# Two pool products emptied ahead of weight splits, and one group's running sums moved, in a two-block recurrent and attention kernel

## The chip, the cores and the metric

The kernel runs on one core of a Trainium2 chip. The metric is the device time of one execution in microseconds (us). Before the change it is 1481.7 us, the median of three runs (1480.57 to 1482.08).

## The reference, cut to what matters

Two transformer-like blocks follow each other on 528 positions (16 meta tokens and 512 real ones) of width 1024, in 32-bit floats. Only the first half of the first block matters here:

```python
z = rmsnorm(h, norm1_g)
q, fl, iv, og, pin, ga, gb = jnp.split(z @ w_in, SPLITS, axis=-1)
o_a = hgrn2_mixer(q, fl + b_f, iv, og, lb_all, head_norm_g)   # 8 heads, gated recurrence
o_b = pool_mixer(pin, w_pool, pool_scale)                     # 4 groups of 128 channels
mix = sigmoid(ga) * (o_a @ w_branch_a) + sigmoid(gb) * (o_b @ w_branch_b)

# pool_mixer, for group g with window w = (2, 4, 8, 16)[g]:
#   d = trailing_mean(pin[:, g], w) - pin[:, g];  y = (d @ w_pool[g]) * pool_scale
```

## The kernel before, in words

**Precision.** Each 32-bit operand of a large product is split in a high and a low part; a product is the sum of three TensorE products (high·high, high·low, low·high). Weights come in units of 1024 KB: SyncE loads a unit to `raw`, ScalarE copies it to `whi` (the high part), and VectorE subtracts to get `wlo` (`w_low`, line 1900). TensorE may start a tile only when `wlo` of its unit is done (`w_lo`).

**Tiles and slots.** The projection `z @ w_in` is worked off in tiles of 128 output channels by all positions; a tile is eight steps of three products in two halves, 48 matmuls of 258 or 264 columns (line 908). Its result lies in one of two PSUM slots, taken in turn. A tile may start only after the one before in its slot was emptied (`acc_free`). The four pool products (`("pool", g)`, six matmuls each) take their turns in the same two slots. A pool product is emptied twice over: ScalarE writes the scaled high part `obhi`, then VectorE writes the low part `oblo` (`pool_out`, line 2155), and only that frees the slot.

**The order.** It is one list, `order`, that TensorE, ScalarE and VectorE each walk through by hand-written rules. The recurrence works on pairs of heads p = 0 to 3; its ten steps (i = 0 to 9) are hung as hooks on the tiles. In the stretch around the change the tiles are, with their hooks (p, i) in brackets: og0 (1,4), pool0, og1 (1,5), pool1, og2 (1,6), pool2, og3 (1,7) and (1,8), q6 (1,9) and (2,0), q7 (2,1), pool3, f6 (2,2), f7 (2,3), g00 (2,4), and so on (q6 is `("q", 6)`, g00 is `("g", 0, 0)`). The slots: og1, og2, og3, q7 and f6 use slot 0; pool1, pool2, q6, pool3 and f7 use slot 1.

**TensorE's side.** After a tile it carries out the hooks. Steps (p,1) to (p,7) are small matmuls on `E` (lines 1009 to 1043) that wait for `mul_ready`. Step (p,9) (lines 1075 and 1077) starts with a wait for `qd_ready`, and at its first chunk for `c0_copied`; it signals `o_done`. Step (p+1,0) follows (transposes, line 988).

**VectorE's side, in its order.** At og1: hooks, then `pool_prep(2)` (running sums on line 2168, the mean minus the frame on line 2174, the split to `pdhi` and `pdlo` on lines 2182 and 2184, with the recurrence's products of step 6 in between), then the low part of the weights of unit q6. At pool1: `pool_out(1)`. At og2: differences of step 7 (lines 2046 and 2047), a masked copy, products of step 7 (lines 2058 and 2059). At pool2: `pool_out(2)`. At og3: a masked copy, the low part of the weights of unit f6, and the differences of step (2,0) (lines 2038 and 2041). At q6: copies of scores (lines 2073 to 2083), the five small masked copies to `sc0` that end in `c0_copied` (lines 2144 and 2149), the products of step (2,0), and, once `o_done` of p = 1 is there, the differences of step (2,1). Then `pool_prep(3)`: four running sums, products of step (2,1), which wait for ScalarE's exponentials, the mean, the split. At q7: differences and products of step (2,2), and the low part of the weights of unit g00. At pool3: `pool_out(3)`.

A unit is handed to `w_low` at the last tile of the unit two places ahead in the order; the dictionary `end_of` says at which tile:

```python
w_low(*end_of.get(name, ()))
```

ScalarE's own walk through the list (the high parts of the weights at `first_of`, table loads, exponentials, `obhi`) isn't touched.

Of the kernel before, what the change touches and what calls it, by code (L numbers as in the profile page):

```python
# [34 lines left out]
T = NM + SEQ  # L35
# [8 lines left out]
POOL_WINDOWS = (2, 4, 8, 16)  # L44
PADC = 16
# [247 lines left out]
def build_program(nc: bass.Bass, a, out):  # L293
# [3 lines left out]
    with ctx:  # L297
        def at(name, shape, dt, offset):
            size = int(np.prod(shape[1:])) * {F32: 4, F32R: 4, BF16: 2, U8: 1}[dt]
            return nc.alloc_sbuf_tensor_at(name, shape, dt, offset=offset), offset + size  # L300
# [54 lines left out]
        og, e = at("og", [P, 4, T], F32, e)  # L355
        pin, e = at("pin", [P, 4, T + PADC], F32, e)
# [12 lines left out]
        pp = [at(f"pp{i}", [P, T + PADC], F32, GOFF + i * (T + PADC) * 4)[0] for i in range(2)]  # L369
# [216 lines left out]
        def acc_late(name):  # L586
            s = 2 * pl.tile[name][0]
            return PS[:, s:s + 2, 0:LHALF]

        def halves(t):  # L590
            return t.rearrange("p (a b) -> p a b", a=2)

        def late(t):
            return t[:, LATE:T]

        def tile_done(eng, name):
            eng.wait_ge(pe_mark, pl.tile[name][1])

        def tile_free(ins, name):
            ins.then_inc(acc_free[pl.tile[name][0]], 1)  # L600

        def tile_freed(eng, name):
            slot, _, uses = pl.tile[name]
            eng.wait_ge(acc_free[slot], uses + 1)
# [42 lines left out]
        first_of, end_of = {}, {}  # L647
# [172 lines left out]
        def _(pe):  # L820
# [39 lines left out]
            def gemm_steps(name, free=True):  # L860
# [5 lines left out]
                s = pl.slot[p.unit]  # L866
                pe.wait_ge(w_lo, p.unit + 1)
                slot, _, uses = pl.tile[name]
                if p.first and uses and free:
                    pe.wait_ge(acc_free[slot], uses)  # L870
# [516 lines left out]
        def _(act):  # L1387
# [25 lines left out]
            def w_high(*units):  # L1413

                for u in units:
                    assert u == n_high[0], (u, n_high)
                    n_high[0] += 1
                    _, kt, cols = pl.units[u]
                    s_ = pl.slot[u]
                    act.wait_ge(w_landed[s_], landed_at[u])  # L1420
                    A_(hi[s_][:, 0:kt * cols], raw[s_][:, 0:kt * cols], ACT.Copy).then_inc(w_hi, 1)
# [457 lines left out]
        def _(dve):  # L1879
# [3 lines left out]
            def tick(ins):  # L1883
                steps[0] += 1
                ins.then_inc(dve_step, 1)

            def settle():
                dve.wait_ge(dve_step, steps[0])
# [3 lines left out]
            def w_low(*units):  # L1892

                for u in units:
                    assert u == n_low[0], (u, n_low)
                    n_low[0] += 1
                    _, kt, cols = pl.units[u]
                    s_, n_ = pl.slot[u], kt * cols
                    dve.wait_ge(w_hi, u + 1)
                    V.tensor_tensor(lo[s_][:, 0:n_], raw[s_][:, 0:n_], hi[s_][:, 0:n_].bitcast(F32), ALU.subtract)\  # L1900
                     .then_inc(w_lo, 1)
# [104 lines left out]
            def values_out(j, turned, copied, dst, m, c0):  # L2006
                dve.wait_ge(turned, j + 1)
                r0 = 96 if m == QB else 0
                V.tensor_copy(dst[r0:r0 + NM, m, P * j:P * (j + 1)], PS[0:NM, 5, 0:P]).then_inc(copied, 1)
                V.tensor_copy(dst[:, c0:c0 + 4, P * j:P * (j + 1)], PS[:, 4, :].rearrange("p (c f) -> p c f", c=4))\  # L2010
                 .then_inc(copied, 1)
# [140 lines left out]
            def pool_out(g):  # L2152
                n = ("pool", g)
                dve.wait_ge(obhi_ready, g + 1)
                tile_free(V.scalar_tensor_tensor(out=halves(late(oblo[:, g, :])), in0=acc_late(n), scalar=col("pscale", g),
                                                 in1=halves(late(obhi[:, g, :].bitcast(F32))), op0=ALU.mult,
                                                 op1=ALU.subtract), n)

            def pool_prep(g, between=lambda: None):

                W_, w = T + PADC, POOL_WINDOWS[g]
                tile_freed(dve, ("pin", g))
                src = pin[:, g, :]
                cur = src
                for s in range(g + 1):
                    d = 1 << s
                    dst = pp[s % 2]
                    tick(V.tensor_tensor(dst[:, 2 * d - 1:W_], cur[:, 2 * d - 1:W_], cur[:, d - 1:W_ - d], ALU.add))
                    settle()
                    cur = dst  # L2170
                between()
                dst = pp[(g + 1) % 2]
                c0 = PADC + w - 1
                tick(V.scalar_tensor_tensor(out=dst[:, c0:W_], in0=cur[:, c0:W_], scalar=1.0 / w, in1=src[:, c0:W_],
                                            op0=ALU.mult, op1=ALU.subtract))
                tick(V.tensor_tensor(dst[:, PADC:c0], cur[:, PADC:c0], inv_n[:, 0:w - 1], ALU.mult))
                settle()
                tick(V.tensor_tensor(dst[:, PADC:c0], dst[:, PADC:c0], src[:, PADC:c0], ALU.subtract))
                settle()
                if g >= 2:  # L2180
                    tile_done(dve, ("pool", g - 2))
                tick(V.tensor_copy(pdhi[g % 2][:, :], dst[:, PADC:W_]))
                settle()
                V.tensor_tensor(pdlo[g % 2][:, :], dst[:, PADC:W_], pdhi[g % 2][:, :].bitcast(F32), ALU.subtract)\
                 .then_inc(pd_ready, 1)
                dve.wait_ge(pd_ready, g + 1)

            def branch_b(k):
                n = ("y", 0, k)
                tile_done(dve, n)  # L2190
                tile_freed(dve, ("g", 0, k))
                tile_free(V.tensor_tensor(halves(late(mix[:, k, :])), acc_late(n), halves(late(mix[:, k, :])), ALU.mult), n)

            waiting = []
            for name, hooks in order:
                kind, h = name[0:2]
                p, hh = h // 2, h % 2
                for step in (hooks if kind != "y" else []):
                    rec_step(*step)
                p_, i_ = hooks[-1] if hooks else (0, 0)  # L2200
                if waiting and name != ("v", 1):
                    values_out(waiting.pop(0), v_turned, v_copied, vtok1, 0, 1)
                if kind == "v":
                    waiting.append(h)
                if name == ("y", 0, 0):
                    rec_step(3, 9)
                    branch_b(0)
                if kind == "f":
                    tile_freed(dve, name)
                    if p >= 2:  # L2210
                        dve.wait_ge(o_done, 2 * (p - 1))
                    f, k_ = av[p % 2][:, hh, :], kf[p % 2][:, hh, :]
                    tick(V.tensor_scalar(f, k_, omlb[:, h:h + 1], lb[:, h:h + 1], ALU.mult, ALU.add))
                    settle()
                    V.tensor_scalar(k_, f, -1.0, 1.0, ALU.mult, ALU.add).then_inc(f_ready, 1)
                    if 1 <= i_ <= 6:
                        rec_step(p_, i_ + 1, "products")
                        rec_step(p_, i_ + 1, "state and differences")
                    dve.wait_ge(ln_ready, h + 1)
                    V.tensor_tensor_scan(f, rmask[:, :], f, 0.0, ALU.mult, ALU.add).then_inc(a_ready, 1)  # L2220
                if name == ("pin", 2):
                    dve.wait_ge(spilled, 16)
                    pool_prep(0)
                elif name == ("q", 4):
                    pool_prep(1)
                elif name in (("og", 1), ("q", 6)):
                    pool_prep(2 if kind == "og" else 3, lambda: rec_step(p_, i_ + 1, "products"))
                elif kind == "pool":
                    pool_out(h)
                if kind != "f" and name != ("og", 1) and 1 <= i_ <= 6:  # L2230
                    rec_step(p_, i_ + 1, "products")
                w_low(*end_of.get(name, ()))
                if i_ == 8 and p_ < 3:
                    rec_step(p_ + 1, 0, "differences")
# [449 lines left out]
```

## Time and profile before

| | us |
|---|---|
| median of 3 runs | 1481.7 (1480.57 to 1482.08) |
| profiled execution, its own time | 1483.7 |
| its span, first to last instruction | 1481.5 |
| TensorE busy in the span | 1460.8 |
| VectorE busy | 839.4 |
| ScalarE busy | 699.8 |
| mean granted TensorE clock | 0.997 of full |

The span is what the trace shows; the 2.2 us between it and the execution's own time lie outside of the first and last instruction. Busy shares are means over stages; a wait counts only where TensorE, which is busy nearly all the time, stands still for it.

### The profile page before, as it was taken

Reading aid. Unit: us, or ns where it says so; the run is one execution under the profiler, and the core shown is the slowest. Engines: PE = TensorE matmul, PEld = TensorE weight load, DVE = VectorE, ACT = ScalarE, POOL = GpSimd, SP = SyncE. Lnnn points to the kernel's source line nnn. Section 1 sums busy time; section 2 is a strip of 40 time slices with the busy share of each in tenths; the row PEclk is TensorE's granted clock in tenths of the full one; section 3 lists DMA queues with packets and bytes.
Section 4 is the critical chain, followed back from the end, with each engine's and each line's share of the span. In section 5 each row is a group of like instructions: output and inputs, shape, how many; then the busy total and the mean of one; then the engine's idle time right before and its main releaser. Section 6 shows DMA issues by size and latency. Waiting matters only on the chain.

```text
span 1481.5 us, 26488 instructions
## 1 busy us (share of the span) xinstructions
PE 1460.8 (99%) x11375; PEld 1293.3 (87%) x11375; DVE 839.4 (57%) x1365; ACT 699.8 (47%) x1041; POOL 51.9 (4%) x150
## 2 busy tenths in 40 slices
PE   7999999999999999999999999999999999999998
PEld 7999999999999899898888777788899888778888
DVE  6487877764656566653344888542223666643343
ACT  6475877853443222222333677532122877743232
POOL 0000000000000000000000021000000111100000
PEclk9999999999999999999999999999999999999999
DMA  6222121124422233223234300222223111123222
GB/s 233 97 65 88 58 85 61 59 72 139 134 86 87 85 100 100 86 86 106 81 100 108 63 29 1 77 90 91 85 86 91 58 58 58 58 90 95 86 94 78
DMA packets 134871, 126.03 MB, mean 85 GB/s; under 512 B 24521, under 2 KB 132836, under 8 KB 134500
## 3 DMA queue, kind: packets, MB, share of 16 engines
q1 hardware_dynamic: 134084, 120.39, 26.1%
q0 software_dynamic: 656, 3.96, 0.9%
q8 instruction: 90, 1.47, 0.4%
q14 instruction: 25, 0.20, 0.0%
q10 hardware_dynamic: 16, 0.00, 0.0%
HBM read 119.69 MB, written 4.26 MB: 84 GB/s over the span
## 4 chain that ended last, share of the span: by engine, by line
PE 91%; DVE 3%; ACT 3%; issue 2%; DMA 0%; SPq 0%; DVEq 0%; ACTq 0%
PE PS L908 79%; PE PS L1242 2%; PE PS L1209 2%; PE PS L1190 2%; DVE wlo L1900 1%; ACT whi L1396 1%; PE PS L1194 1%; PE PS L1193 1%; PE PS L1019 1%; ACT Pm L1396 1%; DMA xt<-in_x 0%; PE PS L1219 0%; ACT L1396 0%; PE PS L975 0%; PE PS L1075 0%
## 5 line engine op out<-in xcount | busy, mean ns | idle before, releaser
L908 PE MATMUL PS<-zhi,whi 128*128 128x258 f32 (+2 forms) x1856 | 487.8, 320 | 2.5 <-DVE prm L1978 0.8
L908 PE MATMUL PS<-zhi,wlo 128*128 128x258 f32 (+2 forms) x1856 | 477.6, 315 | 0.0
L908 PE MATMUL PS<-zlo,whi 128*128 128x258 f32 (+2 forms) x1856 | 476.2, 315 | 0.6 <-DVE zlo L1948 0.6
L908 PEld LDWEIGHTS PS<-zhi,whi 128*128 128x128 f32 x1856 | 307.5, 189 | 27.4 <-issue 1.9
L908 PEld LDWEIGHTS PS<-zhi,wlo 128*128 128x128 f32 x1856 | 306.2, 189 | 22.3
L908 PEld LDWEIGHTS PS<-zlo,whi 128*128 128x128 f32 x1856 | 306.5, 189 | 20.9 <-DVE zlo L1948 0.8
L1900 DVE TENSOR_TENSOR wlo<-raw,whi 128x2048 fp32r<-128x2048 f32 (+2 forms) x114 | 247.8, 2174 | 119.3 <-ACT whi L1396 119.1
L1396 ACT ACTIVATE whi<-raw 128x2048 fp32r<-128x2048 f32 (+2 forms) x114 | 207.5, 1820 | 151.5 <-DMA raw<-in_w_up 57.3
L1396 ACT ACTIVATE Pm<-Pm,small 128x144 f32<-128x144 f32 (+3 forms) x128 | 73.1, 572 | 38.1 <-DVE small L2463 37.7
L2463 DVE CUSTOM_DVE_ANT_0 Pm<-PS,cmask 128x144 f32<-128x144 f32 (+3 forms) x128 | 62.9, 503 | 29.1 <-PE PS L1194 17.2
L908 PE MATMUL PS<-glo,whi 128*128 128x512 f32 x176 | 69.9, 397 | 0.0
L908 PE MATMUL PS<-ghi,whi 128*128 128x512 f32 x176 | 69.7, 396 | 0.0
L908 PE MATMUL PS<-ghi,wlo 128*128 128x512 f32 x176 | 69.1, 392 | 0.0
L1396 ACT ACTIVATE nsq<-PS 128x512 f32<-128x512 f32 x32 | 19.1, 596 | 102.5 <-PE PS L908 101.4
L1209 PE MATMUL PS<-ident,Pm 128*128 128x128 f32 x320 | 54.0, 274 | 1.8 <-ACT PT L1396 1.0
L803 POOL COPY Pe<-Pm 128x16 f32<-128x16 f32 x128 | 44.9, 354 | 224.7 <-ACT Pm L1396 216.8
L1209 PEld LDWEIGHTS PS<-ident,Pm 128*128 128x128 f32 x320 | 39.9, 140 | 14.7 <-ACT PT L1396 3.3
L1396 ACT ACT_TABLE_LOAD x37 | 47.5, 1283 | 7.8 <-PE PS L908 7.2
L908 PE MATMUL PS<-ylo,whi 128*128 128x512 f32 x128 | 51.1, 399 | 0.0
L908 PE MATMUL PS<-yhi,whi 128*128 128x512 f32 x128 | 50.4, 394 | 0.0
L908 PE MATMUL PS<-yhi,wlo 128*128 128x512 f32 x128 | 50.2, 392 | 0.0
L1396 ACT ACTIVATE E<-E 128x1056 f32<-128x1056 f32 (+2 forms) x32 | 33.5, 1048 | 31.7 <-DVE E L2047 26.7
(361 smaller groups left out, 2094.6 us busy)
## 6 DMA issues: line engine op xcount, KB each, us to landing
raw<-in_w_in SPq DMA_DIRECT2D x50, 1024.0 KB, 5.2
raw<-in_w_up SPq DMA_DIRECT2D x22, 1024.0 KB, 5.1
raw<-in_w_out SPq DMA_DIRECT2D x8, 1024.0 KB, 5.1
raw<-in_w_down SPq DMA_DIRECT2D x8, 1024.0 KB, 5.1
raw<-in_w_br_mla SPq DMA_DIRECT2D x4, 1024.0 KB, 5.1
raw<-in_w_br_fox SPq DMA_DIRECT2D x4, 1024.0 KB, 5.1
raw<-in_w_down SPq DMA_DIRECT2D x4, 768.0 KB, 4.5
hspill<-hT SPq DMA_DIRECT2D x1, 2112.0 KB, 7.6
```

Of the source, the lines that this page charges most:

```text
L803: nc.gpsimd.tensor_copy(Pe[h % 2][:, 32 * i:32 * i + NM], Pm[h % 2][:, o_:o_ + NM])\
L908: ins = mm(o_, l_, r_, start=first, stop=last)
L1019: ins = mm(dst.rearrange("p (n b) -> p n b", b=half), e[:, hh, t0 + r:t0 + r + 32], rhs, start=True, stop=True)
L1190: ins = mm(dst, qh[h % 2][:, t0:t0 + P], kh[h % 4][:, c0:c1], start=True, stop=True)
L1193: mm(dst, xqa[i_][:, t0:t0 + P], xka[i_][:, c0:c1], start=True, stop=False)
L1194: ins = mm(dst, xqb[i_][:, t0:t0 + P], xkb[i_][:, c0:c1], start=False, stop=True)
L1209: ins = tr(PS[:, 2 + g % 2, P * x:P * (x + 1)], Pm[h % 2][:, o_:o_ + P], ident[:, :])
L1242: mm(PS[64 * r:64 * r + 64, 7, P * j:SEQ], vtok[:, j, v0:v0 + DV], PT[r][:, G_COL[j]:G_COL[j] + G_N[j]], start=j == 0, stop=False, skip_gr ...
L1396: return nc.scalar.activation(out_, in_, func, **kw)
L1900: V.tensor_tensor(lo[s_][:, 0:n_], raw[s_][:, 0:n_], hi[s_][:, 0:n_].bitcast(F32), ALU.subtract)\
L2463: V.tensor_tensor_reduce(out=cut(Pm[h % 2][:, ATT_OFF[i]:ATT_OFF[i] + ATT_N[i]]), in0=s_view(i), in1=cut(cmask[:, T - ATT_N[i]:T]), op0=AL ...
```

## The change

VectorE's instructions are the same in kind and number; only their order changes.

- The low part of unit q6's weights moves from og1 to pool1, behind `pool_out(1)`.
- The low part of unit g00's weights moves from q7 to pool3, behind `pool_out(3)`.
- The low part of unit f6's weights moves from og3 to q6, behind all of `pool_prep(3)`.
- The four running sums of group 3 move from `pool_prep(3)` at q6 to og3, where the split of unit f6 stood.

```diff
-            def pool_prep(g, between=lambda: None):
+            def pool_sums(g):
 
-                W_, w = T + PADC, POOL_WINDOWS[g]
+                W_ = T + PADC
                 tile_freed(dve, ("pin", g))
                 src = pin[:, g, :]
                 cur = src
...
                     settle()
                     cur = dst
+
+            def pool_prep(g, between=lambda: None):
+
+                W_, w = T + PADC, POOL_WINDOWS[g]
+                if g < 3:
+                    pool_sums(g)
+                src, cur = pin[:, g, :], pp[g % 2]
                 between()
...
+            for early, later in ((("og", 1), ("pool", 1)), (("q", 7), ("pool", 3)), (("og", 3), ("q", 6))):
+                end_of[later] = end_of.pop(early)
             waiting = []
...
                     pool_prep(2 if kind == "og" else 3, lambda: rec_step(p_, i_ + 1, "products"))
+                elif name == ("og", 3):
+                    pool_sums(3)
                 elif kind == "pool":
                     pool_out(h)
```

## Rows read from the trace of the kernel before

**Rows 1.** The page's first part: busy us (share of the span) xinstructions.

```profile
PE 1460.8 (99%) x11375; PEld 1293.3 (87%) x11375; DVE 839.4 (57%) x1365; ACT 699.8 (47%) x1041; POOL 51.9 (4%) x150
```

**Rows 2.** Waits of TensorE: who waited for whom, total us, times, longest.

```profile
PE PS L908 <- DVE oblo L2155: 2.1, 1, 2.1
PE PS L908 <- DVE pdlo L2184: 0.7, 1, 0.7
PE PS L908 <- ACT qf L1396: 0.3, 1, 0.3
```

**Rows 3.** Stretches: length, busy us of each engine, then granted clock, DMA share, GB/s.

```profile
30.00:203.00 173.00, 169.47 (x2440) 165.14 (x2440) 129.18 (x205) 112.17 (x121) 0.00 (x0) 1.00 0.28 88
203.50:206.50 3.00, 3.00 (x15) 3.00 (x15) 0.89 (x2) 2.65 (x3) 0.00 (x0) 0.50 0.41 142
207.00:1460.00 1253.00, 1249.30 (x8642) 1088.63 (x8641) 681.09 (x1110) 560.48 (x867) 50.56 (x138) 1.00 0.27 81
```

**Rows 4.** Timeline of TensorE, 174 to 218: start us, us, instructions, [idle before <-releaser].

```profile
174.56 0.70 PE L1024 MATMUL PS<-E 128*32 128x32 f32 x32
177.32 0.48 PE L908 MATMUL PS<-pdhi,wphi 128*128 128x258 f32 x2 [2.06 <-DVE oblo L2155]
...
191.23 0.29 PE L1075 MATMUL PS<-sc,vtok 16*64 16x16 f32 x4
...
200.13 0.23 PE L1009 MATMUL PS<-E 128*16 128x8 f32 x3
...
202.01 0.51 PE L908 MATMUL PS<-pdhi,wphi 128*128 128x258 f32 x2 [0.69 <-DVE pdlo L2184]
...
217.89 0.23 PE L1009 MATMUL PS<-E 128*16 128x8 f32 x3
```

**Rows 5.** Timeline of VectorE, 174 to 191.

```profile
174.21 2.29 DVE L1900 TENSOR_TENSOR wlo<-raw,whi 128x2048 fp32r<-128x2048 f32 x1
176.42 0.75 DVE L2155 SCALAR_TENSOR_TENSOR oblo<-PS,prm,obhi 128x516 fp32r<-128x516 f32 x1
177.09 0.68 DVE L2046 TENSOR_TENSOR E<-av 128x512 f32<-128x512 f32 x1
...
181.88 0.76 DVE L2155 SCALAR_TENSOR_TENSOR oblo<-PS,prm,obhi 128x516 fp32r<-128x516 f32 x1 [1.08 <-ACT obhi L1396]
...
183.17 2.27 DVE L1900 TENSOR_TENSOR wlo<-raw,whi 128x2048 fp32r<-128x2048 f32 x1
185.37 0.18 DVE L2038 TENSOR_TENSOR E<-av 128x32 f32<-128x32 f32 x1
...
190.81 0.18 DVE L2149 COPY_PREDICATED sc<-lvl,PS 16x32 f32<-16x32 uint8 x1
```

**Rows 6.** Timeline of VectorE, 193 to 217.

```profile
193.50 0.71 DVE L2046 TENSOR_TENSOR E<-av 128x528 f32<-128x528 f32 x1 [1.59 <-PE PS L1077]
...
194.75 0.72 DVE L2168 TENSOR_TENSOR pp<-pin 128x543 f32<-128x543 f32 x1
195.50 2.22 DVE L2168 TENSOR_TENSOR pp<-pp 128x541 f32<-128x541 f32 x3
198.52 0.71 DVE L2058 TENSOR_TENSOR E<-E,qf 128x528 f32<-128x528 f32 x1 [0.79 <-ACT E L1396]
...
201.25 0.71 DVE L2184 TENSOR_TENSOR pdlo<-pp,pdhi 128x528 fp32r<-128x528 f32 x1
...
205.61 0.71 DVE L2058 TENSOR_TENSOR E<-E,qf 128x528 f32<-128x528 f32 x1 [2.29 <-ACT E L1396]
...
209.07 0.75 DVE L2155 SCALAR_TENSOR_TENSOR oblo<-PS,prm,obhi 128x516 fp32r<-128x516 f32 x1
...
214.42 0.55 DVE L2213 TENSOR_SCALAR av<-kf,small 128x528 f32<-128x528 f32 x1 [1.93 <-ACT kf L1396]
...
215.97 0.70 DVE L2059 TENSOR_TENSOR E<-E,kf 128x528 f32<-128x528 f32 x1
```

**Rows 7.** Chain that ended last: tiles f6, f7 and g00 (start us, us, what).

```profile
203.33 7.59 PE PS L908 x48
...
211.92 6.04 PE PS L908 x48
218.96 6.02 PE PS L908 x48
```

## The prediction

> **What bounds the kernel now.** Read the page's first part, TensorE's waits, and then the timelines of the few microseconds in which the change sits. TensorE is busy 1460.8 of 1481.5 us [rows 1]: any time that the change wins or loses is a shift of TensorE's instructions, and what VectorE does matters only where TensorE stands still for it. In the touched stretch TensorE waits three times [rows 2]: 2.1 us for `oblo`, 0.7 us for `pdlo`, 0.3 us for `qf`. There is one more loss. The granted clock is 1.00 from 30 to 203, 0.50 from 203.5 to 206.5, and 1.00 again from 207 to 1460 [rows 3], so tile f6 takes 7.59 us where f7 takes 6.04 [rows 7]: 1.55 us at the lower level (1.2 instead of 2.4 GHz). All that the change could win here is 2.1 + 0.7 + 0.3 + 1.55 = 4.6 us.
>
> **Part 1, `pool_out(1)` ahead of the split of unit q6.** TensorE's small matmuls of step (1,6) start at 174.56 and end at 175.26; pool2 starts at 177.32, 2.06 us later, because slot 1 is freed by the `oblo` of 176.42 [rows 4, 5]. That `oblo` stood behind the split of 174.21. The swap starts it at 174.21 and ends it at 174.96, before TensorE needs it. TensorE reaches pool2 at 175.2, 2.1 us early. VectorE's pair still ends where the differences start, at 177.09, so from there VectorE is as before: `oblo` of pool2 at 181.88 (it waits for ScalarE's `obhi`) and og3's work at 183.17 [rows 5]. Slot 1 is free for q6 at 182.64 + 0.15; TensorE wants it at 183.1 (its tile times unchanged). No wait there, by 0.3 us. Split q6 ends 0.7 us later than before, 6 us ahead of its need.
>
> **Part 2, sums in place of the split of f6 at og3.** The sums take from 194.75 to 197.72, 3.0 us [rows 6]. The split that they replace takes 2.2 (183.17 to the next start, 185.37) [rows 5]. From there to the end of the last copy to `sc0` (190.81 + 0.18 = 190.99) VectorE has no idle time, so `c0_copied` comes 0.8 us later, at 191.79. Step (1,9) waits for it; it starts at 191.23 now, right behind its tile, only 0.24 us after the copy's end [rows 4]. With Part 1 TensorE is there at 191.23 − 2.1 = 189.1 and finds nothing: it stands for 2.8 us and starts at 191.79 + 0.15 = 191.94 (0.15 is what lies between the end of `oblo` at 177.17 and pool2 at 177.32). So the 2.1 us of Part 1 are lost again (2.0 of them would be lost even without Part 2), and 0.7 us on top. A split or a sum in place of the other between two idle ends would cost nothing; here the cover is gone. Bounds: 0.65 to 0.85, by a release of 0.05 (`pdlo` at 201.96 to pool3 at 202.01) or 0.15 and sums of 2.95 to 3.0.
>
> **Part 3, the same sums removed at q6.** The differences of 193.50 follow `o_done`, so they shift by 0.7 to 194.2. The sums that stood behind them were followed by 0.79 us of idle before the products of 198.52, which wait for ScalarE's exponential [rows 6]. ScalarE's chain (the copy of `oT`, two table loads, silu, exponential) also starts at `o_done`, so the products go to 199.2, not earlier. Taking 3.0 us of sums away makes the idle time longer and nothing else. `pdlo`, 201.25 + 0.71 = 201.96 now, ends at 202.67. TensorE still waits for it before pool3.
>
> **Part 4, the split of f6 behind `pool_prep(3)`.** It was done at 185.4; f6 starts at 203.33 [rows 7]. Now it can only start when `pdlo` ends: 202.70 + 2.27 = 204.97, and f6 starts at 205.1. This is the new wait, 1.8 us after 203.33 (0.7 of it carried from Part 2, 1.1 new); the 0.3 us for `qf` disappear in it. Behind the split VectorE has the differences of step (2,2), 202.0 now, 204.9 then; ScalarE's exponential of them, and the products of 205.61, which come at about 207.3. TensorE needs these products only after f6. Lower end for this part: 0 beyond the carried 0.7, if VectorE got the split done in its idle time ahead of the products; its order forbids it. Upper end 1.2. I take 1.1, the durations being shown.
>
> **Part 5, `pool_out(3)` ahead of the split of g00.** The `oblo` of 209.07 frees slot 1 for f7, which starts at 211.92, and no wait stands there [rows 6, 7]: worth 0 now. It is of use against Part 4: VectorE is 1.7 us late at the products, the `oblo` comes at 208.6 (not 209.07 + 1.7), and what follows it is 1.6 us late. The split of g00 ends at 211.4; g00 starts at 218.96. ScalarE's `kf` follows the same delay: 214.42 becomes about 216.05.
>
> **The sum.** −2.1 (Part 1) + 2.1 (stands before step (1,9)) + 0.7 (Part 2) + 0 (Part 3) + 1.1 (Part 4) + 0 (Part 5) = +1.8 us at the start of f6. If f6 again takes 7.6 us, f7, g00 and all behind shift by 1.8: VectorE is late by 1.6 and so isn't the bound. From 230 on TensorE meets nothing that isn't itself counted from TensorE's own tiles, so the shift stays to the end. Profiled execution: 1483.7 + 1.8 = 1485.5. The median of the runs stands 2.0 under the profiled execution; the forecast is 1481.7 + 1.8 = 1483.5 us, a loss of 0.12%. I take 0.2% (3.0 us) as what can be told from no change, so this counts as no change.
>
> **The clock, row and rule.** The row: TensorE stood 2.06 us at 175.26 and the clock stayed at 1.00; it fell to 0.50 after the small matmuls of 200.13, a stop of 0.69, pool3 and a stop of 0.33 [rows 2 to 4]. So one stop of 2 us didn't do it, and thin work with short stops did. The Trainium skill ("TensorE: Matmul & The Clock Gate", section "HAM oscillation — how this bites in real kernels") says that waits between bursts put the array back to half clock and that the next burst starts cold. By this rule the new stand of 2.8 us ahead of step (1,9) speaks against the change; by the row it may pass. With the rule the forecast would be that of rival A, with the row that of the sum.
>
> **Rivals.** *A, the clock halves at step (1,9) (slower).* TensorE stands 2.8 us, longer than any stop in the stretch; if the clock then falls, step (1,9), from 191.23 to the differences' start at 193.50 (2.25 us), loses between 0.5 and 2.2 us, and everything hangs on its `o_done`: differences, exponential, `pdlo`, split, f6. Middle +1.7: 1483.5 + 1.7 = 1485.2 us. Half clock in tile q7 behind it costs nothing, for TensorE waits for `pdlo` and the split anyway. For it: the length of the stop, and that step's matmuls are short. Against: the stop at 175.26. It decides from 1.2 us of extra time up. *B, the clock doesn't fall at f6.* The stops around it change place. f6 then takes 6.0 instead of 7.6, and TensorE would be at step (2,3) ahead of VectorE: its products now end at 216.67 for a start at 217.89 [rows 4, 6], 1.2 us of slack against a delay of 1.6. Shift +0.5: 1482.2 us. *C, faster: the copies to `sc0` don't hold step (1,9).* If the release of step (1,9) were another, earlier one, and VectorE's work from 183 to 191 had slack, the 2.1 us of Part 1 would stay up to `o_done`, `pdlo` would come 2.1 us earlier and the split end at 202.1, ahead of f6: −2.1, and −1.55 more with a full clock: 1479.6 or 1478.0 us. For it: no wait is recorded there now. Against: TensorE comes just 0.24 us after the copy's end. *D, the reorder does nothing that TensorE sees* (±0.4, 1481.7): needs both new waits to be absent; Part 4's is too well priced.
>
> **How the numbers follow.** The sum 0.53 (its own range 1482.8 to 1484.4), A 0.26, B 0.12, C 0.04, D 0.05. Slower by over 0.2% means above 1484.7: three quarters of A, and a little of the sum's tail, 0.23. Faster by over 0.2% means under 1478.7: half of C, and what I have not seen, 0.03. Same 0.74. The range reaches from B's lower side to A's upper half: 1481.3 to 1486.0.
>
> **What would show it.** After: no wait for `oblo` before pool2 (start near 175.2); a new stop of TensorE of some 2.8 us at line 1075, released by VectorE's `sc0` copy (line 2149), start near 191.9; VectorE idle for 3.7 us before the products near 199.2; a wait of TensorE for `wlo` (line 1900) of some 1.5 us before f6, start near 205.1; g00 starting near 220.7. The granted clock from 189 to 197 decides between the sum and A, that from 205 to 209 between the sum and B. The prediction is wrong if step (1,9) starts near 189, or f6 before 203.5.

## The result, and the profile after

The changed kernel takes 1483.59 us (median of 19 runs, 1482.17 to 1486.41) against 1481.62 us (19 runs, 1480.41 to 1482.96): 1.97 us or 0.13% slower, ratio 1.0015 with a 95% interval of 1.0008 to 1.0022. The forecast was 1483.5. The profiled execution took 1483.2 us with a span of 1481.0; for it the forecast was 1485.5.

That span is shorter than the one of before, although the kernel is slower. Most of this comes from the start: step (1,6) of TensorE begins at 173.23 in the new trace and at 174.56 in the old [rows 4], in instructions that the change doesn't touch. So the traces are compared by what lies between that step (the 32 matmuls of line 1024, called *the mark* below) and a later instruction, not by the time since the start. A *stand* below is time in which TensorE does nothing.

The page's first part and TensorE's waits in the touched stretch:

```profile
PE 1460.0 (99%) x11375; PEld 1292.7 (87%) x11375; DVE 839.2 (57%) x1365; ACT 700.1 (47%) x1041; POOL 52.1 (4%) x150
```

```profile
PE PS L1075 <- issue: 2.5, 1, 2.5
PE PS L908 <- DVE wlo L1900: 1.1, 1, 1.1
PE PS L1009 <- DVE E L2059: 0.2, 1, 0.2
```

The three waits of before [rows 2], 3.1 us in all, are gone. In their place are 3.8 us of others, the two large ones where they were forecast. "issue" is the trace's word for a wait whose releaser it doesn't name; VectorE's timeline gives it. TensorE (the marked step, pool2, steps (1,9), (2,0), (2,1), pool3, f6, step (2,3)):

```profile
173.23 0.70 PE L1024 MATMUL PS<-E 128*32 128x32 f32 x32
173.86 0.51 PE L908 MATMUL PS<-pdhi,wphi 128*128 128x258 f32 x2
...
190.45 0.29 PE L1075 MATMUL PS<-sc,vtok 16*64 16x16 f32 x4 [2.54 <-issue]
...
193.27 1.88 PE L988 MATMUL PS<-ident,E 128*16 128x128 f32 x8
...
200.97 0.23 PE L1009 MATMUL PS<-E 128*16 128x8 f32 x3
...
202.08 0.51 PE L908 MATMUL PS<-pdhi,wphi 128*128 128x258 f32 x2
...
204.15 0.51 PE L908 MATMUL PS<-zhi,whi 128*128 128x264 f32 x2 [1.08 <-DVE wlo L1900]
...
217.59 0.23 PE L1009 MATMUL PS<-E 128*16 128x8 f32 x3 [0.20 <-DVE E L2059]
```

VectorE:

```profile
172.84 0.76 DVE L2155 SCALAR_TENSOR_TENSOR oblo<-PS,prm,obhi 128x516 fp32r<-128x516 f32 x1
173.51 2.28 DVE L1900 TENSOR_TENSOR wlo<-raw,whi 128x2048 fp32r<-128x2048 f32 x1
...
182.55 2.22 DVE L2168 TENSOR_TENSOR pp<-pp 128x541 f32<-128x541 f32 x3
184.80 0.19 DVE L2038 TENSOR_TENSOR E<-av 128x32 f32<-128x32 f32 x1
...
190.16 0.18 DVE L2149 COPY_PREDICATED sc<-lvl,PS 16x32 f32<-16x32 uint8 x1
...
193.38 0.71 DVE L2046 TENSOR_TENSOR E<-av 128x528 f32<-128x528 f32 x1 [2.11 <-PE PS L1077]
...
198.32 0.71 DVE L2058 TENSOR_TENSOR E<-E,qf 128x528 f32<-128x528 f32 x1 [3.62 <-ACT E L1396]
...
201.80 2.29 DVE L1900 TENSOR_TENSOR wlo<-raw,whi 128x2048 fp32r<-128x2048 f32 x1
```

What is to be seen: `oblo` of pool1 ends at 173.60 and pool2 starts at 173.86 without a wait; the copy to `sc0` ends at 190.34 and step (1,9) starts 0.11 us later; the products wait 3.62 us for ScalarE in the idle time that the sums left; the split of f6 ends at 204.09 and f6 starts at 204.15. And the clock, as stretches (columns as in [rows 3]):

```profile
192.00:195.00 3.00, 3.00 (x22) 2.59 (x19) 1.33 (x2) 1.61 (x2) 0.00 (x0) 0.50 0.00 0
196.00:1460.00 1264.00, 1259.01 (x8793) 1097.90 (x8793) 689.28 (x1122) 570.60 (x879) 50.71 (x138) 1.00 0.26 81
```

It fell to the lower level inside step (1,9), behind the new stand, and not at f6, where it was low before [rows 3]. Step (1,9) took 2.82 us up to the transposes instead of some 2.17 (190.55 to 192.72 in the third-move run below).

Start of each step counted from the mark, in us, for all kernels of this study (one profiled execution each; the last column says where the granted clock was 0.50):

| kernel | step (1,9) | f6 | step (2,3) | half clock at |
|---|---|---|---|---|
| before | 16.67 | 28.77 | 43.33 | f6 |
| changed | 17.22 | 30.92 | 44.36 | step (1,9), start of q7 |
| pool1 first only | 16.41 | 30.11 | 43.51 | step (1,9) |
| pool3 first only | 18.14 | 30.24 | 43.64 | pool2, og3 |
| third move only | 17.23 | 30.26 | 43.71 | none |
| changed, f6's split in idle time | 17.21 | 31.14 | 44.53 | step (1,9), q7, longer |
| sums at q6, f6's split late | 15.52 | 28.63 | 42.09 | none |
| sums and split both at og3 | 19.42 | 33.12 | 47.67 | step (1,9) and f6 |
| f6's split behind products of (2,0) | 15.51 | 27.62 | 41.03 | none |
| the same, copies first | 14.61 | 26.71 | 40.11 | none |

The last column of times has a trap. The execution of before lost 1.5 us at f6 to the clock, between the last two steps of this table, and it took 2.0 us more than the median of its kernel. A kernel that kept the full clock at f6 looks over 1 us better at step (2,3) than against an execution of before that would have kept it too: the third move alone is 0.38 us late there and 1.49 at f6, and its runs are 1.6 us slower.

### The profile page after: what moved, and what is told of

Its sections match the earlier page's. It is cut to its first block, busy times and chain, and to the rows that moved or that the text cites. A ratio compares the mean times of both kernels' runs of the same rounds, so it can differ in the third digit from the quotient of the medians.

```text
span 1481.0 us, 26487 instructions
## 1 busy us (share of the span) xinstructions
PE 1460.0 (99%) x11375; PEld 1292.7 (87%) x11375; DVE 839.2 (57%) x1365; ACT 700.1 (47%) x1041; POOL 52.1 (4%) x150
## 3 DMA queue, kind: packets, MB, share of 16 engines
q8 instruction: 90, 1.47, 0.4%
## 4 chain that ended last, share of the span: by engine, by line
PE 93%; DVE 3%; ACT 3%; issue 1%; DMA 0%; SPq 0%; DVEq 0%; ACTq 0%
PE PS L908 81%; PE PS L1242 2%; PE PS L1209 2%; PE PS L1190 2%; PE PS L1019 1%; DVE wlo L1900 1%; PE PS L1194 1%; PE PS L1193 1%; ACT Pm L1396 1%; PE PS L1219 0%; DMA xt<-in_x 0%; PE PS L1075 0%; PE PS L975 0%; ACT whi L1396 0%; DVE zlo L1948 0%
```

## The experiments

All were timed against the kernel before on the same chip, 11 runs each against 33. There were two sets, on two chips. In the first (pool1 first, the third move, f6's split in idle time, first best kernel) the median of before was 1481.78 us; in the second (pool3 first, both at og3, sums at q6, second best kernel) it was 1482.36 us. The diffs of the third move, of f6's split in idle time and of both at og3 are against the changed kernel, the others against the kernel before.

**Pool1 first only.**

```diff
+            for early, later in ((("og", 1), ("pool", 1)),):
+                end_of[later] = end_of.pop(early)
```

> Only Part 1: pool_out(1) ahead of the split of unit q6; the rest as before. Theory (serial release): the 2.06 us wait before pool2 goes, but c0_copied ends where it did, so TensorE stands about 2.0 us before step (1,9), which starts only 0.1 us earlier: -0.1 us against before (same). Rival (the wait before pool2 was a real 2.1 us): -2.1 us. A loss of 0.5 to 1 us on top would be the halved clock behind the new stand.

Measured 1481.57 us, −0.21, ratio 0.9998 (0.9989 to 1.0007). TensorE:

```profile
173.25 0.70 PE L1024 MATMUL PS<-E 128*32 128x32 f32 x32
173.87 0.51 PE L908 MATMUL PS<-pdhi,wphi 128*128 128x258 f32 x2
...
189.66 0.29 PE L1075 MATMUL PS<-sc,vtok 16*64 16x16 f32 x4 [1.74 <-issue]
...
193.43 1.04 PE L988 MATMUL PS<-ident,E 128*16 128x128 f32 x8
```

The wait of 2.06 us is gone and a stand of 1.74 us is there in its stead; from the mark, step (1,9) starts 0.26 us earlier than before. A stop was moved, not taken away: the 2.1 us are not a gain as long as `c0_copied` comes when it does. In this execution step (1,9) ran at half clock (granted 0.51 from 190 to 193) and took 3.77 us, so the differences behind it start late and f6 too.

**The third move only** (sums to og3, split of f6 behind `pool_prep(3)`).

```diff
-            for early, later in ((("og", 1), ("pool", 1)), (("q", 7), ("pool", 3)), (("og", 3), ("q", 6))):
+            for early, later in ((("og", 3), ("q", 6)),):
```

> Only the third move: the sums of group 3 at og3 in place of the split of unit f6, that split behind pool_prep(3); no swap at pool1 or pool3. Theory: step (1,9) +0.7, f6 waits for its split, +1.1 more and a further 0.1 to 0.3 downstream, because pool_out(3) stands behind the split of g00 again: +1.8 to +2.0 us. The wait before pool2 (2.06 us) stays and the stand before step (1,9) is only 0.7 us, so the clock shouldn't fall there. Rival (the loss of the change comes from the clock behind its long stand): about +1.0 us or less.

Measured 1483.4 us, +1.6, ratio 1.0014 (1.0005 to 1.0023): nearly the whole loss of the change. Its trace is the cleanest, the granted clock is 1.00 from 174 to 1460:

```profile
174.00:1460.00 1286.00, 1277.61 (x9050) 1116.34 (x9049) 706.13 (x1150) 583.19 (x894) 50.58 (x138) 1.00 0.26 81
```

```profile
PE PS L908 <- DVE oblo L2155: 2.0, 1, 2.0
PE PS L908 <- DVE wlo L1900: 1.3, 1, 1.3
PE PS L908 <- DVE pdlo L2191: 0.6, 1, 0.6
PE PS L1075 <- issue: 0.5, 1, 0.5
```

```profile
190.27 0.18 DVE L2149 COPY_PREDICATED sc<-lvl,PS 16x32 f32<-16x32 uint8 x1
190.55 0.29 PE L1075 MATMUL PS<-sc,vtok 16*64 16x16 f32 x4 [0.55 <-issue]
203.58 0.51 PE L908 MATMUL PS<-zhi,whi 128*128 128x264 f32 x2 [1.34 <-DVE wlo L1900]
```

Step (1,9) is 0.56 us late and f6 1.49, at full clock: no clock loss is needed to make the kernel slower. The time by itself wouldn't exclude the rival, for the interval reaches from +0.7 to +3.4 us; the trace does. The expected +1.8 to +2.0 is a little above the +1.6.

**Pool3 first only.**

```diff
+            for early, later in ((("q", 7), ("pool", 3)),):
+                end_of[later] = end_of.pop(early)
```

> Only Part 5: pool_out(3) ahead of the split of unit g00. Theory: f7 doesn't wait for slot 1 before or after, so no change: 0 us, within 0.3. Rival (that slot's release held f7): -0.3 to -2.2 us.

Measured 1482.62 us, +0.26, ratio 0.9999 (0.999 to 1.0007): nothing. Its profiled execution shows something else. Up to pool2 TensorE's work and VectorE's are those of before, the stop is the same, but behind it the clock fell, which in the execution of before it didn't:

```profile
176.56 0.73 PE L908 MATMUL PS<-pdhi,wphi 128*128 128x258 f32 x2 [2.05 <-DVE oblo L2155]
```

```profile
177.00:180.00 3.00, 3.00 (x16) 3.00 (x15) 2.52 (x5) 2.35 (x2) 0.00 (x0) 0.50 0.00 0
```

**The changed kernel, f6's split in VectorE's idle time** (behind the differences of step (2,1), ahead of its products).

```diff
-            for early, later in ((("og", 1), ("pool", 1)), (("q", 7), ("pool", 3)), (("og", 3), ("q", 6))):
+            for early, later in ((("og", 1), ("pool", 1)), (("q", 7), ("pool", 3)),):
                 end_of[later] = end_of.pop(early)
+            f6_units = end_of.pop(("og", 3))
...
+                    def between():
+                        if kind == "q":
+                            w_low(*f6_units)
+                        rec_step(p_, i_ + 1, "products")
+                    pool_prep(2 if kind == "og" else 3, between)
```

> The changed kernel, but the split of unit f6 stands in VectorE's idle time of 3.6 us, after the sums' old place and ahead of the products of step (2,1), instead of behind pool_prep(3). Theory: the wait of 1.1 us for wlo before f6 goes, the shift left is the 0.7 us of step (1,9) and what its clock costs: +0.7 us over before plus up to 1 for the clock, 0.9 to 1.2 under the changed kernel. Rival (f6 is held by ScalarE and pdlo anyway): equal to the changed kernel, +2.0.

Measured 1483.06 us, +1.28, ratio 1.0009 (1.0 to 1.0018), 0.7 less than the change's own +1.97. The wait for `wlo` is gone from TensorE's list; this is all that is left:

```profile
PE PS L1075 <- issue: 2.5, 1, 2.5
PE PS L1009 <- DVE E L2059: 0.2, 1, 0.2
```

The 0.7 us is less than the 0.9 to 1.2 expected, and it rests on medians of different sets of runs, and the two intervals overlap, so that this kernel gains anything over the change is not shown. In the profiled execution the clock was low for longer than in any other, 0.50 for all of 192 to 198, so its f6 doesn't start earlier than that of the change:

```profile
192.00:198.00 6.00, 6.00 (x47) 5.55 (x47) 2.72 (x4) 2.23 (x4) 0.00 (x0) 0.50 0.00 0
```

**Both at og3** (both swaps, the sums and the split of f6 at og3: 3.0 us more ahead of `c0_copied` than before).

```diff
-            for early, later in ((("og", 1), ("pool", 1)), (("q", 7), ("pool", 3)), (("og", 3), ("q", 6))):
+            for early, later in ((("og", 1), ("pool", 1)), (("q", 7), ("pool", 3))):
```

> Both swaps, and at og3 both the sums and the split of unit f6: VectorE has 3.0 us more work ahead of c0_copied than before. Theory (every microsecond at og3 goes to step (1,9)): TensorE stands 5.0 us, step (1,9) starts 2.9 us later than before, f6 waits for nothing new: +2.9 us, and 1 to 2.2 us more where the clock halves behind the stand: +3.9 to +5. Rival (there is slack behind step (1,9), so only the late split of f6 cost): +1 us or less.

Measured 1485.93 us, +3.57, ratio 1.0024 (1.0015 to 1.0033).

```profile
193.46 0.29 PE L1075 MATMUL PS<-sc,vtok 16*64 16x16 f32 x4 [4.74 <-issue]
```

Step (1,9) is 2.75 us later than before for 3.0 us of work, and the kernel 3.57 us slower. So there is next to no slack between VectorE's work at og3 and step (1,9) (the 0.24 us of before): the rival falls. The time is under the +3.9 to +5 of the theory, which had put 1 to 2.2 us more on the clock.

**The sums at q6, f6's split late** (both swaps, the split of f6 behind `pool_prep(3)`, the sums where they were).

```diff
+            for early, later in ((("og", 1), ("pool", 1)), (("q", 7), ("pool", 3)), (("og", 3), ("q", 6))):
+                end_of[later] = end_of.pop(early)
```

> Both swaps and the split of unit f6 behind pool_prep(3), as in the change, but the sums stay in pool_prep(3). Theory: with nothing at og3 step (1,9) starts about 1.2 us earlier than before, as in the last run (it is ScalarE's exponential that holds it then, not c0_copied), pdlo follows by as much, and f6 still waits 1.5 us more for its split than it would: about +0.2 us over before in f6's start, and the clock's loss at f6 may go or stay: -0.5 to +0.5 us. Rival (the sums' place doesn't matter, only the late split does): +1.5 us, as with the third move alone.

Measured 1481.96 us, −0.40, ratio 0.9999 (0.999 to 1.0008). Against the change this kernel differs in the place of the sums alone. Step (1,9) is 1.7 us earlier than in the change, f6 2.3, and the wait for f6's split is the same 1.34 us as in the third move alone:

```profile
190.13 0.29 PE L1075 MATMUL PS<-sc,vtok 16*64 16x16 f32 x4 [0.84 <-issue]
203.24 0.51 PE L908 MATMUL PS<-zhi,whi 128*128 128x264 f32 x2 [1.34 <-DVE wlo L1900]
```

The theory's −0.5 to +0.5 is met and the rival's +1.5 isn't: with the late split kept, taking the sums out of og3 undoes the loss.

**Best kernel, first version:** both swaps, sums in `pool_prep(3)`, the split of f6 at q6 behind the products of step (2,0), where VectorE waits for `o_done`.

```diff
                     mul(0)
+                    if p == 2:
+                        w_low(*end_of.pop(("og", 3)))
                     sub(1)
...
+            for early, later in ((("og", 1), ("pool", 1)), (("q", 7), ("pool", 3)),):
+                end_of[later] = end_of.pop(early)
...
-                w_low(*end_of.get(name, ()))
+                w_low(*(end_of.get(name, ()) if name != ("og", 3) else ()))
```

> Both swaps; the sums of group 3 back in pool_prep(3); the split of unit f6 taken out of og3 and put at q6 between the products of step (2,0) and the differences of step (2,1), where VectorE waits for o_done. Theory: c0_copied comes 2.2 us earlier, at 188.8, before TensorE needs it (189.1), so the 2.1 us of Part 1 stay: no stand before step (1,9), pdlo and f6 2.1 us earlier: -2.1 us against before. Rival (the order of the two tiles' work isn't the limit; something else releases step (1,9) at its old time): -0.1 us or more.

Measured 1479.98 us, −1.80, ratio 0.9989 (0.998 to 0.9998): faster than before, if only just clear of the noise. Of the two sides of the expectation the theory holds, but not in full: step (1,9) starts 1.16 us earlier and not 2.1, with a stand of 0.83 us left. VectorE's timeline (below the line of TensorE) names the next wait in the row, the product with the queries (line 2140 here), which needs an exponential of ScalarE:

```profile
188.88 0.29 PE L1075 MATMUL PS<-sc,vtok 16*64 16x16 f32 x4 [0.83 <-issue]
```

```profile
181.94 0.17 DVE L2038 TENSOR_TENSOR E<-av 128x32 f32<-128x32 f32 x1
...
184.95 1.26 DVE L2140 TENSOR_TENSOR E<-E,qf 128x1056 f32<-128x1056 f32 x1 [1.18 <-ACT E L1396]
...
188.60 0.18 DVE L2151 COPY_PREDICATED sc<-lvl,PS 16x32 f32<-16x32 uint8 x1
```

**Best kernel, second version:** the same, and for p = 1 the score copies up to `c0_copied` ahead of that product (the lines shared with the first version are left out).

```diff
+                    def q_decay():
+                        dve.wait_ge(qd_exp, p + 1)
+                        t = E[(b + 8) % 2]
+                        V.tensor_tensor(t[:, :, :], t[:, :, :], q[:, :, :], ALU.mult).then_inc(qd_ready, 1)
+
                     evac(6)
-                    dve.wait_ge(qd_exp, p + 1)
-                    t = E[(b + 8) % 2]
-                    V.tensor_tensor(t[:, :, :], t[:, :, :], q[:, :, :], ALU.mult).then_inc(qd_ready, 1)
+                    if p != 1:
+                        q_decay()
                     evac(7)
...
+                    if p == 1:
+                        q_decay()
```

> The last kernel of the first set (both swaps, sums in place, split of f6 behind the products of step (2,0)), and for the second pair of heads the score copies up to c0_copied ahead of the product with the queries, which waits 1.2 us for ScalarE's exponential. Theory: the remaining stand of 0.8 us before step (1,9) goes: -0.8 us against that kernel, -2.6 against before (1479.2). Rival (the clock's chance decides, the stand of 0.8 us costs nothing on top): -1.8.

Measured 1479.01 us (1478.86 to 1480.2), −3.35, ratio 0.9978 (0.9969 to 0.9986). TensorE has no wait left before step (1,9):

```profile
PE PS L908 <- DVE pdlo L2192: 0.7, 1, 0.7
PE PS L908 <- ACT qf L1396: 0.3, 1, 0.3
PE PS L1009 <- DVE E L2059: 0.2, 1, 0.2
```

```profile
173.71 0.70 PE L1024 MATMUL PS<-E 128*32 128x32 f32 x32
...
188.32 0.29 PE L1075 MATMUL PS<-sc,vtok 16*64 16x16 f32 x4
```

It is 2.06 us earlier there than before, the whole wait of [rows 2]. The granted clock is 1.00 from 20 to 1460 in this and the version before it.

The time fell by more than that, 3.35 us, and by more than the 2.6 expected. The runs with a mean granted clock of 1.000 tell where the rest may come from: four of this kernel took 1478.86 to 1479.36 us, and three of before, in the same set, 1480.89 to 1481.60. Their medians differ by 2.1 us, the wait. The median of all runs of before is 1.3 us above that of its three, while that of this kernel doesn't differ from its four. So some 1.3 us of the gain would be clock losses that before has in many of its executions and this kernel hasn't. That rests on few runs and is not shown.

## Why the prediction was right

**Part 1 (`pool_out(1)` first): −2.1, then +2.0 lost.** Right in both halves. The wait before pool2 is gone in every kernel with the swap; alone it moved step (1,9) by −0.26 us (forecast −0.1) and the time by −0.21, which isn't told from nothing.

**Part 2 (sums in place of a split at og3): +0.7.** The mechanism is right and the size a little too large: +0.56 us at step (1,9). In the third-move run the copies end 0.70 us later from the mark (17.13 against 16.43 us), not 0.8, and the release took 0.10 us, not 0.15 (0.11 in the changed kernel). The stand of the changed kernel was 2.54 us, forecast 2.8.

**Part 3 (sums gone from q6): 0.** Right: the idle time before the products grew from 0.79 to 3.62 us, forecast 3.7.

**Part 4 (late split of f6): +1.1.** Measured without a clock loss in the third-move run: 1.49 − 0.56 = +0.9 us. The wait before f6 there is 1.34 us, forecast 1.5.

**Part 5 (`pool_out(3)` first): 0.** Right.

**The sum.** The forecast was +1.8 at f6; from waits alone it is +1.5. The measured +1.97 us is 0.5 more. In the changed kernel's trace the clock fell inside step (1,9), which took 0.65 us more, and f6 came 2.15 us late; of that 0.65 are the clock's. So the time of 1483.5 was met with a first term slightly too large and no term for the clock. That two errors of opposite sign nearly cancel is luck. That the clock is the 0.5 us is argued from one trace of each kernel, and not shown as a mean over the runs; by the fastest run of each kernel, 1482.17 against 1480.41 us, the loss is 1.76, which would leave less for it.

**Rivals A and B.** They were weighed as alternatives to the sum and both took place in the profiled execution: the clock fell at step (1,9), A's mechanism with +0.65 instead of +1.7 us, and stayed up at f6 as in B. Together they give step (2,3) at +1.03 us from the mark: 0.65 of A and 0.38 for B, forecast 0.5, with the wait of 0.20 us for VectorE's products that B foretold. That is the price against an execution of before that lost 1.5 us at f6, and not the +1.97 of the medians; how often before loses them there isn't known. It is also why the profiled execution took 1483.2 us and not the 1485.5 of the forecast. Here the weighing of row and rule failed. The prediction took one stop of 2.06 us without a fall as what the clock does behind such a stop; in the run with only pool3 first the same stop, 2.05 us, was followed by a granted clock of 0.50 from 177 to 180. The rule had the direction right for the changed kernel, but it doesn't tell the cases apart, for behind stands of 2.00 and 2.06 us the clock stayed up. It was also stretched: in the case that the Trainium skill gives it for ("TensorE: Matmul & The Clock Gate", section "HAM oscillation — how this bites in real kernels") the waits between bursts are longer than the stand here. By the Trainium skill ("TensorE: Matmul & The Clock Gate", section "What's actually happening") the gate isn't tied to where the kernel starts, so that its transition varies from run to run. These traces agree: with unchanged work up to pool2, it fell from pool2 on in one execution and not in another. The wide range of the changed kernel's runs (4.2 us against 2.6) would fit that.

**Rival C** fell: `c0_copied` did hold step (1,9). The last kernels show its price, for once that copy is early, the 2.1 us stay.

**Rival D** fell too: both new waits are in the trace.

## What to carry to other kernels

A wait that is taken away ahead of an engine with almost no idle time is worth only the distance to the next release that didn't move. Before pricing it, read how early each later release comes: here the copy to `sc0` ended 0.24 us before TensorE needed it, and that number, not the 2.06 us of the wait, was the worth of the swap (0.26 us at step (1,9)). Work that is moved should go to where its engine waits for the engine that bounds the kernel; two such places (1.6 us before `o_done`, 1.2 us before a ScalarE exponential) turned a loss of 2 us into a gain of 3.3, of which 2.1 are the wait.

## What the runs showed of the hardware

Stands of TensorE and the clock behind them, one execution each: 1.74 us (fell), 2.05 us (fell), 2.06 us (stayed), 2.00 us (stayed), 2.54 us (fell, twice), 4.74 us (fell), 0.83 and 0.84 us (stayed). Stands of nearly the same length, in the same place, did both. So did the short stops ahead of f6, which the prediction took for the cause of the fall there: 0.69 and 0.33 us in the kernel before (fell) and 0.62 and 0.41 us with both at og3 (fell), but 0.70 and some 0.33 us in the two runs with one swap and in both best kernels (stayed). A single trace can't tell what a stand of some 2 us costs. The loss at a fall is 0.65 us where the clock fell late in step (1,9), and 1.6 us where it fell at its first matmuls (3.77 against 2.17 us).

None of it was caught up further on in these traces. In the run with only pool3 first the fall made step (1,9) 1.47 us late, and f6 was 1.47 us late too. That step (2,3) is only 0.31 us late there is no recovery: before lost its own 1.5 us at f6 in between.
